# Down projection of tiles 0 to 15 by seven block products of sums in place of eight, weight sums formed once and kept in memory, a third slot of split weights

## What is computed

```python
h = rmsnorm(x) * g1
proj = h @ w_in                      # queries, keys, values, indexer, gates
o_a = windowed attention with sinks  # window of 128
o_b = attention over the top 256 keys of an indexer, low-rank keys and values
x = x + (sigmoid(gate_a) * (o_a @ w_a) + sigmoid(gate_b) * (o_b @ w_b)) @ w_out
h2 = rmsnorm(x) * g2
ff = silu(h2 @ w_gate) * (h2 @ w_up)        # 2816 columns: 22 tiles of 128
x = x + ff @ w_down                         # 2816 x 1024
return rmsnorm(x) * g_f
```

## Time and profile before

| | |
|---|---|
| median of 3 runs | 3198.58 us (3197.46 to 3198.94) |
| span of the profiled execution | 3196.7 us |
| TensorE busy | 3156.0 us, 15678 matmuls |
| VectorE busy | 1814.8 us |
| ScalarE busy | 1420.8 us |
| GpSimd busy | 2036.0 us |
| transfers | 392.59 MB |

### The profile page before, as it was taken

The page is one execution under the profiler, slowest core; times in us unless marked ns, Lnnn a source line. Parts: engine busy times, 40 slices in busy tenths (PEclk is TensorE's granted clock), DMA queues, the critical chain, the costliest instruction groups (busy, mean ns, idle before and its releaser), DMA issues.

```text
span 3196.7 us, 44024 instructions
## 1 busy us (share of the span) xinstructions
PE 3156.0 (99%) x15678; PEld 2655.0 (83%) x15678; DVE 1814.8 (57%) x3706; ACT 1420.8 (44%) x2589; POOL 2036.0 (64%) x2201
## 2 busy tenths in 40 slices
PE   9999999999999999999999999999999999999998
PEld 7888888878878888888888888988888799888887
DVE  3335546537565545557666666967868689521111
ACT  3324435435473534337354534837655378320001
POOL 5666766665556666764666676366767922666676
PEclk9999999999999999999999999999999999999999
DMA  5765455355615333331533334163333500533332
GB/s 152 198 167 172 119 154 157 103 157 163 209 35 182 102 112 107 108 125 57 201 104 116 103 102 138 28 238 103 98 109 112 171 23 17 180 91 99 95 103 99
DMA packets 464201, 392.59 MB, mean 123 GB/s; under 512 B 29264, under 2 KB 394064, under 8 KB 463344
## 3 DMA queue, kind: packets, MB, share of 16 engines
q1 hardware_dynamic: 442544, 345.56, 36.0%
q10 hardware_dynamic: 21440, 44.22, 3.7%
HBM read 323.76 MB, written 62.81 MB: 121 GB/s over the span
## 4 chain that ended last, share of the span: by engine, by line
PE 92%; POOL 2%; ACT 2%; DVE 2%; issue 1%; DMA 1%; SPq 0%; POOLq 0%; ACTq 0%; DVEq 0%
PE BANK L1049 22%; PE BANK L1051 21%; PE BANK L1050 21%; PE LP L1049 4%; PE LP L1051 4%; PE LP L1050 4%; PE BANK L1330 3%; PE BANK L1355 2%; PE LP L1166 2%; PE LP L1165 2%; PE LP L1310 2%; PE LP L1311 2%; PE BANK L1357 2%; POOL WLO L986 1%; POOL WHI L984 1%
## 5 line engine op out<-in xcount | busy, mean ns | idle before, releaser
L986 POOL TENSOR_TENSOR WLO<-WRAW,WHI 128x512 fp32r<-128x512 f32 x912 | 1213.3, 1330 | 76.0
L984 POOL TENSOR_SCALAR WHI<-WRAW 128x512 fp32r<-128x512 f32 x912 | 639.6, 701 | 776.1 <-PE BANK L1051 622.1
L1049 PE MATMUL BANK<-H2hi,WHI 128*128 128x512 f32 x1376 | 538.7, 392 | 1.1 <-POOL WLO L986 1.1
L1050 PE MATMUL BANK<-H2lo,WHI 128*128 128x512 f32 x1376 | 535.9, 389 | 0.0
L1051 PE MATMUL BANK<-H2hi,WLO 128*128 128x512 f32 x1376 | 535.8, 389 | 0.0
L1049 PE MATMUL BANK<-HThi,WHI 128*128 128x512 f32 (+1 forms) x1024 | 405.1, 396 | 0.8 <-DVE QS L2044 0.5
L1050 PE MATMUL BANK<-HTlo,WHI 128*128 128x512 f32 (+1 forms) x1024 | 399.4, 390 | 0.0
L1051 PE MATMUL BANK<-HThi,WLO 128*128 128x512 f32 (+1 forms) x1024 | 399.3, 390 | 0.0
L1751 ACT ACTIVATE MASK<-SCD,THR 128x896 bf16<-128x896 f32 (+5 forms) x186 | 281.9, 1516 | 191.8 <-DVE THR L2104 164.6
L1051 PEld LDWEIGHTS BANK<-H2hi,WLO 128*128 128x128 f32 x1376 | 258.3, 188 | 54.4
L1049 PEld LDWEIGHTS BANK<-H2hi,WHI 128*128 128x128 f32 x1376 | 258.6, 188 | 53.3 <-issue 1.3
(11 more groups left out here) (314 smaller groups left out, 6457.6 us busy)
## 6 DMA issues: line engine op xcount, KB each, us to landing
WRAW<-in_w_in SPq DMA_DIRECT2D x124, 512.0 KB, 4.2
WRAW<-in_w_ffn_gate SPq DMA_DIRECT2D x88, 512.0 KB, 3.8
WRAW<-in_w_ffn_up SPq DMA_DIRECT2D x88, 512.0 KB, 3.8
WRAW<-in_w_ffn_down SPq DMA_DIRECT2D x88, 512.0 KB, 3.5
qsp<-QS SPq DMA_DIRECT2D x32, 512.0 KB, 5.8
WRAW<-in_w_out SPq DMA_DIRECT2D x32, 512.0 KB, 4.6
gates<-GS ACTq DMA_DIRECT2D x62, 256.0 KB, 2.2
GL<-gates ACTq DMA_DIRECT2D x48, 256.0 KB, 4.5
```

Of the source, the lines that this page charges most:

```text
L984: nc.gpsimd.tensor_scalar(hi, raw, 1.0, 1.0, ALU.mult, ALU.mult).then_inc(w_hi, 1)
L986: nc.gpsimd.tensor_tensor(lo, raw, hi.bitcast(f32), ALU.subtract).then_inc(w_split, 1)
L1049: nc.tensor.matmul(dst, whi, mhi, start=first, stop=False)
L1050: nc.tensor.matmul(dst, whi, mlo, start=False, stop=False)
```

## The change

Tiles 0 to 15 are taken in four quads of four tiles (`QUADS`). For two neighbouring tiles of `ff` (even and odd) and the two halves of the 512 rows of the block and of the 1024 output columns, the down projection is a product of 2 x 2 blocks; it is computed as seven products of sums (`PRODUCTS`) in place of eight. In a quad each product takes two such pairs of tiles (kk = 0, 1) and two row tiles: 12 matmuls.

- Operands from `ff`: three of the four blocks and four sums are needed in split form, seven in all (`FShi`, `FSlo`, 256 rows each): operand 0 is the even tile's first half, 1 and 2 the odd tile's halves, 3 to 6 sums and differences (`FSUM`). VectorE forms the sums and all low parts, ScalarE the high parts (`low_parts`, `high_parts`).
- Operands from `w_ffn_down`: products 11, 22 and 21 use the blocks themselves, which are loaded and split as before (512 KB raw). Products t1 to t4 use sums that are formed once, during block 0's projections (`load_down`, `down_sums`, ScalarE's copy of the high part), written to memory (`tsum`, high and low parts) and later loaded in split form, 2 x 512 KB, straight to `WHI` and `WLO`.
- A third slot of `WHI` and `WLO` is used by tiles 0 to 15 and the products; the slot used longest ago is taken. `issue_order` lets SyncE issue a raw load ahead of the summed load before it.
- Results: products 11, t2, t3 and t4 accumulate in one pair of banks (`chain`, the tile `LP[0]`), t1 and 22 in another (`corner`), 21 in a third (`single`). After each of the seven, VectorE adds the banks as they stand to a different quarter of `X1` (`add_chain`, `add_banks`); TensorE may go on in a bank only when the addition of what it held is done (`down_added`).
- The search keeps 14 slots a part, placed anew (`search_slots`, `look` inside `add_quad`). Several semaphores are merged, to make room for new ones.

The core of the diff:

```diff
+        FShi, FSlo = (at(s, [P, 2, 7, 2 * P], f32r, r3 + 14336 * i) for i, s in enumerate(("FShi", "FSlo")))
+        FSUM = at("FSUM", [P, 4, 2 * P], f32, r3 + 28672)
+        WHI.append(at("WHI2", [P, SLOTS, P], f32r, rX + 32768))
+        WLO.append(at("WLO2", [P, SLOTS, P], f32r, rX + 36864))
...
+        PRODUCTS = (("11", 0), ("t1", 3), ("t2", 4), ("22", 5), ("t3", 6), ("21", 1), ("t4", 2))
+        SUMS = ("t1", "t2", "t3", "t4")
+        QUADS = sum(len(part) for part in PARTS[:-1]) // 4
+        def quad_jobs(b, quad):
...
+            for x, _ in PRODUCTS:
+                if x in SUMS:
+                    jobs.append((("fs", b, quad, x), io["tsum"][quad, SUMS.index(x)]))
+                else:
+                    tiles = io["w_ffn_down"][0][4 * quad * P:4 * (quad + 1) * P, :].rearrange("(k e p) c -> e p k c", e=2, p=P)
+                    half = int(x[1]) - 1
+                    jobs.append((("fs", b, quad, x), tiles[int(x[0]) - 1, :, :, half * ROWS:(half + 1) * ROWS]))
...
+                if i % 4 == 3 and i // 4 < QUADS:
+                    jobs += quad_jobs(b, i // 4)
...
+                third = key[0] == "fs" or key[0] in ("fg", "fu") and key[2] < PARTS[-1][0]
+                w = min((0, 1, 2) if third else (0, 1), key=lambda s: used[s])
...
+                before.append(max(used[w], last_out) if w == 2 else used[w])
...
-                return 1 if at_ - part[0] in ((0, 1, 2, 3, 4, 6), (0, 1, 2, 3, 4, 6), (0, 1))[PARTS.index(part)] else 2
-            return 3 - at_ if phase == "wo" else 2 if last else 3 - 2 * at_
+                return 1 if at_ - part[0] in ((2, 3, 6, 7), (0, 3, 4, 7), (0, 1))[PARTS.index(part)] else 2
+            return 3 - at_ if phase == "wo" else 2 if last else 1
...
+                if summed(key):
...
+                    sp.wait_ge(bank_full, n(bank_full, JOBS[BEFORE[i]][0]))
...
+                    for s, half in enumerate((WHI, WLO)):
+                        sp.dma_start(half[SLOT[i]][:, :, :].bitcast(f32).rearrange("p k c -> p (k c)"), src[s]
+                                     ).then_inc(summed_in[SLOT[i]], 16)
+                    continue
...
+            def down_quad(b, quad):
+                def product(x, operand, dst, first):
...
+                    if summed(key):
+                        pe.wait_ge(summed_in[w], n(summed_in[w], key))
+                    for kk in range(2):
...
+                        even, odd = 4 * quad + 2 * kk, 4 * quad + 2 * kk + 1
+                        if operand < 3:
+                            pe.wait_ge(ff_split, n(ff_split, (b, odd if operand else even)))
+                        else:
+                            pe.wait_ge(sum_split, n(sum_split, (b, even if operand == 6 else odd, operand)))
+                        for r in range(2):
...
+                            last = three(dst[r], FShi[:, kk, operand, c], FSlo[:, kk, operand, c], hi[:, kk, :], lo[:, kk, :],
+                                         first and kk == 0, kk == 1, chained=True)
+                    last.then_inc(bank_full, made(bank_full, key))
+                chain = take("chain", down_added, (b, quad, "t3"), ("chain", b, quad))
...
+                for x, operand in PRODUCTS:
+                    if x == "11":
+                        product(x, operand, chain, True)
+                    if x == "t1":
+                        corner = [take("corner", down_added, (b, quad, "22"), ("corner", b, quad, r))[:, :] for r in range(2)]
+                        product(x, operand, corner, True)
+                    if x == "t2":
+                        pe.wait_ge(down_added, n(down_added, (b, quad, "11")))
+                        product(x, operand, chain, False)
+                    if x == "22":
+                        pe.wait_ge(down_added, n(down_added, (b, quad, "t1")))
+                        product(x, operand, corner, False)
+                    if x == "t3":
+                        pe.wait_ge(down_added, n(down_added, (b, quad, "t2")))
+                        product(x, operand, chain, False)
+                    if x == "21":
+                        single = [take("single", down_added, (b, quad, "21"), ("single", b, quad, r))[:, :] for r in range(2)]
+                        product(x, operand, single, True)
+                    if x == "t4":
+                        pe.wait_ge(down_added, n(down_added, (b, quad, "t3")))
+                        product(x, operand, chain, False)
...
+                def high_parts(i):
+                    kk = i // 2 % 2
...
+                    if i % 2 == 0:
+                        nc.scalar.copy(FShi[:, kk, 0, :], SL[:, 0, 0:2 * P]).then_inc(ff_hi, made(ff_hi, (b, i)))
+                        act.wait_ge(sum_formed, n(sum_formed, (b, i, 6)))
+                        nc.scalar.copy(FShi[:, kk, 6, :], FSUM[:, 3, :]).then_inc(sum_hi, made(sum_hi, (b, i, 6)))
+                    else:
+                        act.wait_ge(sum_formed, n(sum_formed, (b, i, 3)))
+                        nc.scalar.copy(FShi[:, kk, 3, :], FSUM[:, 0, :]).then_inc(sum_hi, made(sum_hi, (b, i, 3)))
+                        act.wait_ge(sum_formed, n(sum_formed, (b, i, 5)))
+                        nc.scalar.copy(FShi[:, kk, 4:6, :], FSUM[:, 1:3, :]).then_inc(sum_hi, made(sum_hi, (b, i, 5)))
+                        nc.scalar.copy(FShi[:, kk, 1:3, :], SL[:, 1, :].rearrange("p (s r) -> p s r", s=2)
+                                       ).then_inc(ff_hi, made(ff_hi, (b, i)))
...
+                def low_parts(i):
...
+                    if i % 2 == 0:
+                        nc.vector.tensor_tensor(FSUM[:, 3, :], ev[:, low], ev[:, high], ALU.subtract
+                                                ).then_inc(sum_formed, made(sum_formed, (b, i, 6)))
+                        dve.wait_ge(ff_hi, n(ff_hi, (b, i)))
+                        nc.vector.tensor_tensor(FSlo[:, kk, 0, :], ev[:, low], FShi[:, kk, 0, :].bitcast(f32), ALU.subtract
+                                                ).then_inc(ff_split, made(ff_split, (b, i)))
+                        dve.wait_ge(sum_hi, n(sum_hi, (b, i, 6)))
+                        nc.vector.tensor_tensor(FSlo[:, kk, 6, :], FSUM[:, 3, :], FShi[:, kk, 6, :].bitcast(f32), ALU.subtract
+                                                ).then_inc(sum_split, made(sum_split, (b, i, 6)))
+                        return
+                    nc.vector.tensor_tensor(FSUM[:, 0, :], ev[:, high], bk[:, high], ALU.add
+                                            ).then_inc(sum_formed, made(sum_formed, (b, i, 3)))
+                    dve.wait_ge(sum_formed, n(sum_formed, (b, i, 3)))
+                    nc.vector.tensor_tensor(FSUM[:, 1, :], FSUM[:, 0, :], ev[:, low], ALU.subtract
+                                            ).then_inc(sum_formed, made(sum_formed, (b, i, 4)))
+                    dve.wait_ge(sum_formed, n(sum_formed, (b, i, 4)))
+                    nc.vector.tensor_tensor(FSUM[:, 2, :], bk[:, low], FSUM[:, 1, :], ALU.subtract
+                                            ).then_inc(sum_formed, made(sum_formed, (b, i, 5)))
+                    dve.wait_ge(sum_hi, n(sum_hi, (b, i, 3)))
+                    nc.vector.tensor_tensor(FSlo[:, kk, 3, :], FSUM[:, 0, :], FShi[:, kk, 3, :].bitcast(f32), ALU.subtract
+                                            ).then_inc(sum_split, made(sum_split, (b, i, 3)))
+                    dve.wait_ge(sum_hi, n(sum_hi, (b, i, 5)))
+                    for s in (4, 5):
+                        nc.vector.tensor_tensor(FSlo[:, kk, s, :], FSUM[:, s - 3, :], FShi[:, kk, s, :].bitcast(f32), ALU.subtract
+                                                ).then_inc(sum_split, made(sum_split, (b, i, s)))
+                    if kk:
+                        add_chain(quad, "11")
+                    dve.wait_ge(ff_hi, n(ff_hi, (b, i)))
+                    nc.vector.tensor_tensor(FSlo[:, kk, 1:3, :], bk.rearrange("p (s r) -> p s r", s=2),
+                                            FShi[:, kk, 1:3, :].bitcast(f32), ALU.subtract).then_inc(ff_split, made(ff_split, (b, i)))
...
+                def add_chain(quad, x):
...
+                    dve.wait_ge(bank_full, n(bank_full, ("fs", b, quad, x)))
+                    c = X1[:, 2 * top:2 * top + 2, half * ROWS:(half + 1) * ROWS]
+                    nc.vector.tensor_tensor(c, LP[0][:, :].rearrange("p (r c) -> p r c", r=2), c, ALU.add
+                                            ).then_inc(down_added, made(down_added, (b, quad, x)))
...
+                def add_quad(quad, part):
+                    add_banks(quad, "t1", (0, 2))
+                    look("fd", part)
+                    add_chain(quad, "t2")
+                    add_banks(quad, "22", (0, 2))
+                    add_chain(quad, "t3")
+                    add_banks(quad, "21", (1, 3))
+                    add_chain(quad, "t4")
...
+                d11, d12, d21, d22 = (DRAW[:, e, half * ROWS:(half + 1) * ROWS] for e in range(2) for half in range(2))
```

(27 more changed lines are left out.)

244 lines of the change are left out of this document (178 added, 66 removed).

## The result

The changed kernel takes 3460.0 us (median of 4 runs, 3458.5 to 3460.5) where the kernel before took 3198.4 beside it: 1.0817 times as long, 95% interval 1.0802 to 1.0832. The forecast was 3363 us in a range of 3240 to 3460: the sign is right, and the time lies at the very edge of the range, 97 us above the forecast.

The account below looks back on a forecast made before the run. TensorE, busy 99% of the span, was taken to bound the kernel before. Blocks 2, 1, 0 and 3 at +71, +40, +23 and 0 and the projection at +30 made +164 on 3198.6: 3363 us, range 3240 to 3460.

Parts of the forecast that it names:

- VectorE's round: Feed-forward quad, end of t4 to next t4: 79.9, 72.2, 63.8 us without contention in blocks 2, 1, 0.
- The rounds: Quad periods with contention in blocks 2, 1, 0, against 68.1 us before: +17.8, +10.1, +5.7 us a quad.
- Legs 1 and 5: Parts of a quad's period: TensorE's gate and up of the next tile, 11.6 us; three products after t2's addition, 8.2.
- Contention: VectorE's 20 new two-SBUF-input operations a quad slowed by GpSimd: 0.3 us each in blocks 1 and 2, 0.5 in block 0.
- the 0.9 of the rival: Full contention, 0.9 us an operation: blocks 2, 1, 0 at +126, +96, +62, in all 3513 us; chance 8%.
- Near attention: Its VectorE work and waits add 9.3 us a quad in block 2, taken as 7.5 as half the waited work is done.
- t1, 22 and t3 products: Sign of being right: TensorE idle before these, put down to VectorE, largest in block 2, near zero in block 3.
- near 90% busy in block 2's parts: Sign of being right: VectorE's busy share in block 2's feed-forward parts near 90%.
- VectorE still waiting for TensorE in block 2: Sign of being wrong: the round would then count legs that overlap, called the likeliest error.
- Block 3: Feed-forward without search beside it: only the products' own pace; gain 11 to loss 17 us, taken as 0.
- The rival of late weights: TensorE waits for summed weights in every block, 8.9 us each, +17 a block; about 3400 us; chance 4%.
- The projection: Block 0's projection, forming weight sums once: 25 MB in some 16 jobs, +30 us taken, 3 to 84 possible.

Follow-up runs that it names:

- narrow search: Changed kernel with two of eight forming rounds, counts of blocks 1 to 3 made 64 columns wide: 3259.3 us, against 3394.4 without the short counts.
- moved steps: Complete changed kernel with two search steps put behind the quad's additions in place of ahead of t1's and t2's: 3405.3 us (1.0643).
- short_two_rounds: Changed kernel with two of eight forming rounds and search counts of blocks 1 to 3 only 64 columns wide: 3259.3 us (1.0190).
- traffic_only: Changed kernel with all eight rounds' transfers, but rounds 2 to 7 without sums, copies and waits for them: 3438.6 us (1.0750).

## Why the prediction was right, and where it was off

- **What bounds it, and which way.** Right. TensorE's saving was at most 43.6 us and it arrives only in block 3; VectorE's round sets blocks 0 to 2, most in block 2. The narrow search (135 us back) and the moved steps (55 us back) show it.
- **The size** was too low, by 97 us in a loss of 261, and the time stayed at the edge of the range by luck: terms that were too high (block 2's idle time, block 3) cover part of those that were too low or missing.
- **The rounds** of 85.9, 78.2 and 73.8 us a quad measured 89.4, 83.8 and 77.9. Their idle time was nearly right in blocks 0 and 1 (35.1 and 52.8 us against 34 and 51) and 15 us too long in block 2. What the sum left out is a term: **the clock**. Legs 1 and 5 of my round took TensorE's pace at 0.227 us a matmul, but behind the long waits the matmuls start 0.43 apart. That is 10, 16 and 25 of the 15, 21 and 30 us more busy time in blocks 0, 1 and 2; 17 to 21 breaks a block, before each of which the last matmul shows its full 0.39, are about 3 more.
- **Contention** at 0.3 and 0.5 us an operation: 0.25 and 0.32 measured. Right in kind, a little high in block 0; the 0.9 of the rival is reached by a single group (L2723 in block 3), by no block's mean.
- **Near attention**, "a VectorE that is late finds half of the waited work done": wrong. VectorE waits 21.1 us for ScalarE's exponentials, not half of 14.7. They start only when VectorE has given the maxima, and so are late by as much as VectorE is. In block 2 other overlaps outweigh it, since the idle time came out lower than summed; which ones is open.
- **Where TensorE waits.** I had named the t1, 22 and t3 products. They are there, but 27.7 of 66.6 us in block 2 belong to near attention. Whether near attention ahead of the search on VectorE and ScalarE would remove that wasn't tried.
- **Two of my signs** were badly chosen. VectorE "near 90% busy in block 2's parts" came out at 76% (270 of 358 us), though the rest of the account held. And VectorE still waiting for TensorE in block 2, which I had called a sign of being wrong, is in the rows (16.8 us at the tiles' multiplication alone). It follows from my own legs 1 and 5, in which VectorE has little to do.
- **Block 3**, forecast 0 with -11 to +17: -7.5. The summed weights land in 3.5 and 4.5 us and no wait of TensorE in the block is put down to them. The rival of late weights is out.
- **The projection**, +30 with 3 to 84: +77, the largest error. The volume of the 25 MB was summed at 41 us too many and then cut, because "prefetched weights hide some". They hid little: six of the eight rounds alone cost 45 us by volume. And a term was missing: the ring of write, sums, load in one set of tiles and one queue, 20 to 25 us. The slower clock is in both (granted 0.84 in 100:260); it is 24 of the 77 us.
- **The sum.** Of the 97 us missing 47 are the projection's and 66 the busy time's in blocks 0 to 2; idle time gives 1, 2 and -15, block 3 -7, and 5 us lie outside these stretches (each rounded).

## What to carry to other kernels

When matmuls are taken out by giving another engine more work, compare the round of that engine between two products that wait for it with TensorE's, not its busy share: here VectorE still held TensorE up at 65% busy. Price every new wait of TensorE twice where it is long, once for the idle time and once for the slower matmuls behind it. Weights formed once aren't free once: in this projection, with the DMA engines 0.7 busy, each MB beyond the first rounds cost 2.5 us, and buffers that are written out before they may be filled again tie the rounds to the writes.

## What the runs showed of the hardware

- The granted clock averaged 0.90 in a stretch in which TensorE was still busy 81% of the time (block 2). Its idle time came in 17 waits of over 0.5 us, the longest 13.1. In block 1 of short_two_rounds, 92% busy with no wait over 6.4 us, it was 0.98.
- In the projection 1 MB of loads and 1 MB of writes cost TensorE the same 2.5 us each, though nothing in block 0's projection waits for the writes of traffic_only's last six rounds. The first two rounds, with 6 MB and their sums, cost 6.8 us in all, so this price doesn't hold from the first MB on. The fullest stretch moved 278 GB/s at a DMA share of 0.86, above the 238 of the earlier trace rows.
- What a VectorE operation with two SBUF inputs costs hangs on whether GpSimd is splitting at that moment: 0.68 and 1.77 us for the same one in block 2. So a mean from one stretch doesn't carry over to another: L2723 takes 0.905 us on average in block 2 and 1.335 in block 3.
